# Convolution input panels multiplied in the wide form: one 512-column product with the high weights in place of two of 256 columns

## What is computed

```python
def short_conv_mixer(h, w_in, w_conv, w_out):      # h: 256 x 1024, w_in: 1024 x 3072
    b_gate, c_gate, v = jnp.split(h @ w_in, 3, axis=-1)
    u = c_gate * v
    conv = causal convolution of u over 3 tokens, per channel, taps w_conv
    return (b_gate * conv) @ w_out
...
for i in range(DEPTH):                              # two layers
    mod = silu(c) @ ada_w[i] + ada_b[i]             # shifts, scales and gates
    h = modulate(x, tok_norm[i], sh1, sc1)
    x = x + g1 * (short_conv_mixer(h) if i == 0 else mla_mixer(h))
    h = modulate(x, ch_norm[i], sh2, sc2)
    x = x + g2 * peer_mixer(h)
```

## Time and profile before

| | us |
|---|---|
| median of 3 runs | 1879.51 |
| lowest and highest | 1877.51, 1880.39 |
| the profiled execution's own time | 1876.5 |
| its span | 1874.7 |
| TensorE busy | 1855.6 (99%) |
| VectorE busy | 1448.8 (77%) |
| GpSimd busy | 1044.1 (56%) |
| ScalarE busy | 999.7 (53%) |

### The profile page before, as it was taken

How to read it: one execution, slowest core, us unless ns; L and a number is a source line. 1 busy time by engine, 2 the same in 40 slices (tenths; PEclk the granted TensorE clock), 3 DMA queues, 4 the chain that set the end, 5 groups by cost and what they waited for, 6 DMA issues and landing times.

```text
span 1874.7 us, 37387 instructions
## 1 busy us (share of the span) xinstructions
PE 1855.6 (99%) x12430; PEld 1645.0 (88%) x12430; DVE 1448.8 (77%) x2801; ACT 999.7 (53%) x1580; POOL 1044.1 (56%) x506
## 2 busy tenths in 40 slices
PE   8999999999999999999999999999999999999998
PEld 7999999888888888887789999988888888888887
DVE  6757998899878977797765489977887678666866
ACT  4354565555555555554455645555555555555553
POOL 3877557767776776100063575677787777773000
PEclk8999999999999999999999999999999999999999
DMA  8987657889888988887633576567787778777764
GB/s 349 361 271 251 209 136 190 229 227 247 234 237 231 277 231 240 252 277 232 230 103 96 179 238 192 137 160 189 179 203 189 190 188 219 189 191 214 230 189 139
DMA packets 222024, 399.45 MB, mean 213 GB/s; under 512 B 84192, under 2 KB 131680, under 8 KB 221536
## 3 DMA queue, kind: packets, MB, share of 16 engines
q1 hardware_dynamic: 137856, 383.21, 63.3%
q0 software_dynamic: 55296, 0.22, 7.1%
q10 hardware_dynamic: 28768, 14.68, 2.7%
HBM read 382.11 MB, written 15.93 MB: 212 GB/s over the span
## 4 chain that ended last, share of the span: by engine, by line
PE 92%; DVE 3%; DMA 2%; ACT 1%; POOL 1%; issue 1%; DVEq 0%; SPq 0%; ACTq 0%; POOLq 0%
PE bank L680 37%; PE bank L665 18%; PE bank L670 10%; PE bank L644 6%; PE bank L649 6%; PE bank L645 6%; PE bank L711 1%; PE bank L699 1%; DMA raw<-in_panels 1%; POOL w_lo L1387 1%; PE bank L727 1%; PE bank L509 1%; DMA raw<-in_v_panels 1%; PE bank L529 1%; PE bank L966 1%
## 5 line engine op out<-in xcount | busy, mean ns | idle before, releaser
L1418 POOL DMA_INDIRECT gates_of_tile<-g_t,place x384 | 765.9, 1995 | 324.0 <-DMA gates_of_tile<-g_t,place 147.6
L1025 ACT CAST w_hi<-raw 128x1024 fp32r<-128x1024 f32 (+1 forms) x603 | 630.5, 1046 | 354.0 <-DMA raw<-in_v_panels 119.5
L1443 DVE TENSOR_TENSOR w_lo<-raw,w_hi 128x1024 fp32r<-128x1024 f32 x488 | 597.2, 1224 | 234.0 <-PE bank L680 114.3
L1387 POOL TENSOR_TENSOR w_lo<-raw,w_hi 128x1024 fp32r<-128x1024 f32 (+2 forms) x115 | 273.1, 2379 | 323.1 <-PE bank L680 179.3
L665 PE MATMUL bank<-act_two,w_hi 128*128 128x512 f32 x1536 | 379.4, 389 | 0.0
L665 PEld LDWEIGHTS bank<-act_two,w_hi 128*128 128x128 f32 x1536 | 288.4, 188 | 59.7
L680 PE MATMUL bank<-w_hi,wt_hi 128*128 128x512 f32 x1024 | 324.4, 397 | 1.8 <-DVE wt_lo L1705 0.9
L680 PE MATMUL bank<-w_lo,wt_hi 128*128 128x512 f32 x1024 | 318.0, 391 | 0.0
L680 PE MATMUL bank<-w_hi,wt_lo 128*128 128x512 f32 x1024 | 317.2, 390 | 0.0
L644 PE MATMUL bank<-act_two,w_hi 128*128 128x256 f32 x984 | 246.4, 288 | 0.0
L645 PE MATMUL bank<-act_two,w_hi 128*128 128x256 f32 x984 | 241.2, 283 | 0.0
(11 more groups left out here) (259 smaller groups left out, 1902.5 us busy)
## 6 DMA issues: line engine op xcount, KB each, us to landing
raw<-in_u_panels SPq DMA_DIRECT2D x256, 512.0 KB, 4.1
raw<-in_v_panels SPq DMA_DIRECT2D x256, 512.0 KB, 4.0
raw<-in_panels SPq DMA_DIRECT2D x81, 512.0 KB, 4.4
ada<-in_ada_rows SPq DMA_DIRECT2D x56, 512.0 KB, 4.8
arena<-in_ada_rows SPq DMA_DIRECT2D x40, 512.0 KB, 7.2
gates_of_tile<-zero ACTq DMA_DIRECT2D x2, 4096.0 KB, 22.6
arena<-gates_of_tile SPq DMA_DIRECT2D x32, 256.0 KB, 4.3
gates_of_tile<-g_t,place POOLq DMA_INDIRECT x384
```

Source lines behind the costliest of these rows:

```text
L1025: nc.scalar.copy(w_hi[:, slot, 0:width], raw[:, slot, 0:width]).then_inc(hi_done, 1)
L1387: pool.tensor_tensor(w_lo[:, lo_slot, 0:width], raw[:, slot, 0:width], w_hi[:, slot, 0:width].bitcast(F32), ALU.subtract).then_inc(lo_done, 1)
L1418: pool.indirect_dma_start(grid, bass.IndirectOffsetOnAxis(place[:, n:n + 1], 0), kept[:, n:n + 1], None, compute_op=ALU.add).then_inc(adde ...
L1443: dve.tensor_tensor(w_lo[:, lo_slot, 0:width], raw[:, slot, 0:width], w_hi[:, slot, 0:width].bitcast(F32), ALU.subtract).then_inc(lo_done, 1)
```

## The change

Panels 2 to 23 of the input product go through a new `wide_conv_panel`: with the high weights 8 matmuls of 512 columns in place of 16 of 256, and the low weights as before. The product is now in two halves of a bank. ScalarE copies the second half to a buffer `conv_lo` (two slots of 128x256, in a part of `ring_g` that nothing else uses at this stage), **behind** the cast of panel p+3, and VectorE adds the first half to it, which releases the bank. Two of each three products had been multiplied straight out of the bank; these now need an add and then the multiply.

```diff
@@ -180,6 +180,7 @@
 
         sq = arena[:, 0:2048]
         c_sb = arena[:, 2048:2048 + T]
+        conv_lo = ring_g[:, 5120:5632].rearrange("p (e n) -> p e n", e=2)
         conv_t = arena[:, 3072:3072 + T]
         sq_sum = arena[:, 3328:3328 + T]
 
@@ -293,6 +294,7 @@
         by_gain = sem("x_by_gain_ready")
         x_ready = sem("x_ready")
         sq_ready = sem("squares_ready")
+        conv_lo_ready = sem("conv_low_half_copied")
         sum_ready = sem("square_sums_ready")
         rms_ready = sem("rms_ready")
         rstd_ready = sem("token_rstd_ready")
@@ -653,6 +655,23 @@
 
                 pe.wait_ge(pan_read[l], nth)
                 hi_then_lo(bank[:, 0:T], stage, j, norm_act)
+
+            def wide_conv_panel(j):
+
+                hi_slot, lo_slot, _, n = ring("conv_in", j)
+                bank = PAN[j % 2]
+                pe.wait_ge(evac["conv_in"], j + 1)
+                pe.wait_ge(hi_done, n)
+                for k in range(KB):
+                    w, a = slice(k * P, (k + 1) * P), slice(k * T, (k + 1) * T)
+                    pe.matmul(bank[:, 0:2 * T], w_hi[:, hi_slot, w], act_two[:, :, a], start=(k == 0), stop=False,
+                              skip_group_check=True)
+                pe.wait_ge(lo_done, n + RAW)
+                for k in range(KB):
+                    w, a = slice(k * P, (k + 1) * P), slice(k * T, (k + 1) * T)
+                    mm = pe.matmul(bank[:, 0:T], w_lo[:, lo_slot, w], act_hi[:, a], start=False, stop=(k == KB - 1),
+                                   skip_group_check=True)
+                mm.then_inc(pan_done, 1)
 
             def wide_u_panel(l, stage, j, unroll, it, nth, bank):
 
@@ -1006,7 +1025,7 @@
             busy(PAN[0], 50)
             first_pair(norm_hi, norm_ready, 0, lambda p: wait_panel("conv_in", p), fill=5)
             for j in range(2, 24):
-                full_panel("conv_in", j)
+                wide_conv_panel(j)
             conv_pair()
             for j in range(2, 8):
                 full_panel("conv_out", j, acts=conv_act)
@@ -1255,7 +1274,11 @@
             for it in range(2):
                 for b in range(4):
                     for j in range(3):
-                        split_hi("conv_in", 12 * it + 3 * b + j + HI_LEAD)
+                        p = 12 * it + 3 * b + j
+                        split_hi("conv_in", p + HI_LEAD)
+                        if p > 1:
+                            act.wait_ge(pan_done, ring("conv_in", p)[3] + HI)
+                            nc.scalar.copy(conv_lo[:, p % 2, :], PAN[p % 2][:, T:2 * T]).then_inc(conv_lo_ready, 1)
                     if it == 0:
                         conv_high(b)
             act.wait_ge(pan_done, ring("conv_in", 23)[3] + HI)
@@ -2037,13 +2060,24 @@
 
                     if b:
                         ada_row(15 + 3 * b, 12, it, 3 * b - 1)
-                    wait_product("conv_in", 12 * it + 3 * b)
-                    dve.tensor_copy(c_sb, PAN[3 * b % 2][:, 0:T]).then_inc(evac["conv_in"], 1)
+                    p = 12 * it + 3 * b
+                    if p == 0:
+                        wait_product("conv_in", p)
+                        dve.tensor_copy(c_sb, PAN[p % 2][:, 0:T]).then_inc(evac["conv_in"], 1)
+                    else:
+                        dve.wait_ge(conv_lo_ready, p - 1)
+                        dve.tensor_tensor(c_sb, PAN[p % 2][:, 0:T], conv_lo[:, p % 2, :], ALU.add).then_inc(evac["conv_in"], 1)
                     ada_row(16 + 3 * b, 12, it, 3 * b)
                     dve.drain()
-                    wait_product("conv_in", 12 * it + 3 * b + 1)
-                    dve.tensor_tensor(u_pad[:, 2:2 + T], PAN[(3 * b + 1) % 2][:, 0:T], c_sb, ALU.mult
-                                      ).then_inc(evac["conv_in"], 1)
+                    p += 1
+                    if p == 1:
+                        wait_product("conv_in", p)
+                        dve.tensor_tensor(u_pad[:, 2:2 + T], PAN[p % 2][:, 0:T], c_sb, ALU.mult).then_inc(evac["conv_in"], 1)
+                    else:
+                        dve.wait_ge(conv_lo_ready, p - 1)
+                        dve.tensor_tensor(conv_t, PAN[p % 2][:, 0:T], conv_lo[:, p % 2, :], ALU.add).then_inc(evac["conv_in"], 1)
+                        dve.drain()
+                        dve.tensor_tensor(u_pad[:, 2:2 + T], conv_t, c_sb, ALU.mult)
                     dve.drain()
                     tap = lambda i: vec[:, it * 4 + V_CONV + i * KB + b:it * 4 + V_CONV + i * KB + b + 1]
                     dve.tensor_scalar(conv_t, u_pad[:, 0:T], tap(0), None, ALU.mult)
@@ -2057,9 +2091,11 @@
                         if b == 3:
                             ada_row(15 + 12, 12, it, 11)
                     dve.drain()
-                    wait_product("conv_in", 12 * it + 3 * b + 2)
-                    dve.tensor_tensor(conv_ps[4 * it + b], PAN[(3 * b + 2) % 2][:, 0:T], conv_t, ALU.mult
-                                      ).then_inc(evac["conv_in"], 1)
+                    p += 1
+                    dve.wait_ge(conv_lo_ready, p - 1)
+                    dve.tensor_tensor(c_sb, PAN[p % 2][:, 0:T], conv_lo[:, p % 2, :], ALU.add).then_inc(evac["conv_in"], 1)
+                    dve.drain()
+                    dve.tensor_tensor(conv_ps[4 * it + b], c_sb, conv_t, ALU.mult)
                     dve.drain()
                     dve.sem_inc(conv_gated, 1)
                     if end:
```

## The result

| | us |
|---|---|
| before, median of 4 runs | 1879.95 (1877.51 to 1881.15) |
| with the change, median of 4 runs | 1891.36 (1890.11 to 1891.89) |
| ratio, 95% interval | 1.0059 [1.0043, 1.0074] |
| the profiled execution of the change | 1891.85, span 1890.1 |

The change makes the kernel 11.4 us slower. The forecast was slower, at 1884.5 with a range to 1888.5: the direction is right, the loss is more than twice the one forecast, and the time lies outside the range.

A forecast was written before the change was run, and what follows sets the result against it. TensorE was taken to bound the kernel, DMAs and GpSimd close behind. Terms +3.5 +1.2 +0.5 -0.2 = +5.0 us took the profiled execution from 1876.5 to 1881.5, the median to 1884.5; range 1880.0 to 1888.5.

The forecast's parts named there:

- TensorE's part: On TensorE over 22 input panels: wide panels take 2.77 us against 2.88, gaining 2.4 us if nothing waits.
- The first wait, panel 4: At panel 4's bank: release waits for cast, copy and add until 53.95, so panel 6 starts 1.1 us later than before.
- L: Time from issue to landing of a panel's DMA: 8.2 us for panel 7, 7.7 taken for the second half.
- The prediction's own sign: TensorE idle about 1.5 us before panel 6's first wide matmul; if absent, the panel 4 step and forecast are wrong.
- The second, panel 5: At panel 5's bank: with the added multiply VectorE frees it at 57.85, so panel 7 starts 2.2 us late.
- The turn in the first half: ScalarE and VectorE ring, 8.7 us per three panels: panel 10 stays 2.2 us late, panel 13 is 3.5 late; +3.5 us.
- The second half: Panels 13 to 22: ring through SyncE's DMA issue, cast, copy and add loses 0.8 us per six panels; +1.2 us.
- GpSimd: GpSimd's subtractions beside 15 new multiplies of two SBUF tiles: each stops GpSimd up to 0.36 us; +0.5, ends 0 and 1.5.
- The clock: Rival: TensorE's pauses drop its clock to 1.2 GHz, 2.4 us more per panel, a few making 1892; chance 0.03.
- The end: At `conv_pair`: TensorE's 0.44 us wait for GpSimd goes, 0.3 us of the last gated block shows; together -0.2 us.
- Rival 3: GpSimd becomes the bound: pauses of 0.36 us on each of 22 subtractions, DMA loads of 9.6 us; +9, 1888.5; chance 0.10.

The follow-up runs named there:

- both edits: The change with the second and third products' sums written to PSUM and ScalarE's copy put ahead of the cast; median 1880.98 us, ratio 0.9996.
- row moved: The kernel with both edits, and block 3's second ada row done behind the gated block, after the third add; median 1880.25 us, ratio 0.9994.
- narrow, two steps in PSUM: The kernel before, narrow matmuls kept, VectorE first copying second and third products from the bank to PSUM, then multiplying; median 1882.16 us, ratio 1.0009.
- the narrow form in two steps: The kernel before, narrow matmuls kept, VectorE copying second and third products out, then multiplying; 1891.52 us with the copy in SBUF, 1882.16 in PSUM.

## Why the prediction was right in direction and wrong in size

- **"TensorE's part"**, -2.4 us: right. Panels that don't wait start 2.79 us apart (2.77 was set), and the kernel with the wide matmuls alone is 2.5 us faster. The rule of "TensorE: Matmul & The Clock Gate" of the Trainium skill, section Back-to-back issue gap, by which the prediction worked out 0.5 us, is not what these rows show; the page gives it for an isolated matmul and says itself that it misses the spacing in a stream of weight loads and matmuls, such as this one.
- **"The first wait, panel 4"**: the mechanism is there, as ScalarE's row at 52.56 shows, but panel 6 came only 0.3 us late against the wide pace, not the 1.5 (53.95 against 52.4) of the text. L was 7.25 us (issued at 44.34, landed at 51.6), not 8.2: the load was not fixed by what lay before it. The prediction's own sign, idle time of TensorE before panel 6, is all but absent: 0.14 us (53.30 to 53.44), not 1.5. By its own words the step on panel 4 is wrong in size.
- **"The second, panel 5"**: in the run with the sums in PSUM panel 7 starts 3.74 us behind panel 6, 0.95 late, near the 1.1 that the text added. In the change it was 3.36, of which 2.66 - 0.43 = 2.23 is one multiply.
- **"The turn in the first half" and "The second half"**, +3.5 and +1.2: near in sum, and that in part by luck. With the sums in PSUM, panel 13 starts 34.91 us after panel 2, 3.2 more than before, and the whole stretch is 4.1 longer, against 4.7. But the parts come in other places than set. Against the kernel before, panel 7 is 0.5 us late and not 2.2, and panel 10, which was to stay as it was, loses 0.9 more. The turn of block 3, with its extra ada row, has the 1.66-us wait before panel 13, the largest of that run. That kernel's median, 1885.47, is close to the 1884.5 forecast: the forecast fits the change without the lock.
- **"GpSimd"**, +0.5 with ends 0 and 1.5: **this step failed**, in direction and in size. It read the earlier trace rows as a pause of GpSimd under VectorE's instruction. It is that only for the one that comes second. Here the second is nearly always VectorE, since a subtraction runs for 2.4 of each 2.9 us and a multiply for 0.43. GpSimd lost 0.1 us, once; VectorE lost 10.85 us in the profiled execution, and as its multiply stands ahead of the next release, the stretch is 7.4 us longer than without these waits, with what they did to the clock. No rival of the prediction has VectorE waiting. Its price in place of +0.5 is the most of the miss. The earlier trace rows shows only the one direction, but a bound for the other could be had from its durations: one whole subtraction, 2.4 us, on each of 15 multiplies, 36 us in all, and at even odds of where one falls some 15 x 0.83 x 1.2 = 15 us of VectorE's time (2.4 of 2.9 us busy, half a subtraction left on average; an estimate from those rows).
- **"The clock"** (rival 4, chance 0.03): it happened once, with a wait of 3.08 us before panel 7, and cost 5.28 - 2.79 = 2.5 us there, about the 2.4 a panel of the text, and 0.4 at panel 8; that rival set a few such panels. Waits of up to 1.86 us elsewhere in the stretch were not followed by it. Without the 2.23 us that one multiply lost, that wait would have been 0.85 us. The 1892 of this rival is near the time measured by luck: it has a few slow panels and no lock.
- **"The end"**, -0.2: wrong, a loss of 1.6 us. From the first matmul of `conv_pair` to the first add of VectorE into `xT` were 5.64 us before (105.30 to 110.94) and are 7.22 now (117.47 to 124.69), with 0.88 us of wait at 120.02 for the last bank. Most of this is the lock again: with the sums in PSUM, and as many instructions, it is 5.92 us, while it is 7.23 with only the copy moved.
- **Rival 3** gave 9 us, for another reason: GpSimd did not become the bound, and the DMAs fell from 349 to 298 GB/s.
- Two slips in the working change little: 57.85 - 55.74 is 2.1 us, not 2.2, and the chances of a loss above 1883.3 add up to 0.5 + 0.10 + 0.03 = 0.63, not 0.61.

SBUF — State Buffer of the Trainium skill, section Who interferes with whom, says that a VectorE instruction with two SBUF inputs contends with a GpSimd instruction that reads SBUF, that the shared port pair is an exclusive lock, and that the order of issue decides who blocks. The traces agree: 0.43 against 2.66 us for VectorE here, 2.41 against 3.81 for GpSimd in the earlier trace rows. The prediction used a page that only says that there is contention, and took one side of it.

**What stays open.** The kernels with both edits and with the row moved have a stretch 1.4 and 2.2 us shorter than before, but no shorter median. The times scatter by more than that, and the record shows with what: the granted clock of the execution. The 60 executions of the kernel before took 1878.0 us on average at a clock of 0.995 (15 of them) and 1883.3 at 0.992 (8). The profiled ones show where it comes from. From the first wide panel of the mixing stage of layer 0 to that of layer 1, which none of the edits touches, they took 933.9 us (before), 934.8 (the change), 934.2 (wide matmuls alone) and 934.5 (row moved), each with a clock of 0.98 between 930 and 1110 us; 938.0 and 938.8 (sums in PSUM, both edits), with 0.96; and 944.9 (narrow, two steps in PSUM; the slowest of its 11 executions), with 0.92. At the same clock the two kernels with both edits are a little faster: 1877.1 at 0.995 (5 executions) and 1881.5 at 0.992 (11), 0.8 and 1.7 us below the kernel before. A straight line through times and clocks of each batch puts the gain at 1.3 us (standard error 0.4 and 0.5). That is an estimate of mine from the runs on record, and it says that a part at least of the shorter stretch reaches the end. Why the clock between 930 and 1110 us differs from one execution to the next is open. Whether a form in which VectorE adds the halves without ScalarE's copy would do better was not tried.

## What to carry to other kernels

Before an operand of a two-tensor VectorE instruction is moved from PSUM to SBUF, look at what GpSimd does at that time: with one operand in PSUM the instruction ran beside it untouched in every run, with both in SBUF it waited for the end of GpSimd's instruction, and here that made a change of +5 us (1885.47 against 1880.28) one of +11. On an engine that works in order, a copy that releases a TensorE bank goes ahead of anything that waits for a DMA. Where TensorE is busy for 99%, work moved to a neighbour has to be priced by the delay of the next release, not by its own microseconds.

## What the runs showed of the hardware

- A 128x256 multiply of two SBUF tiles on VectorE waits for the end of GpSimd's running instruction with SBUF inputs and ends 0.28 to 0.30 us after it, up to 2.66 us in place of 0.43; cutting GpSimd's instruction in two cut the longest to 1.50. With one input in PSUM the same multiply takes 0.43 us while the subtraction runs. GpSimd's instruction is not slowed when it came first; the one that began 0.17 us after a multiply took 2.53 us, not 2.41. I had expected the reverse.
- Waits of 3.08 us (the change) and 2.12 us (the subtraction in two) on TensorE came with the lower clock, 0.50, for most of the panel behind them (5.28 and 4.37 us in place of 2.79); those of up to 1.86 us in the change, and of up to 1.75 in the runs with only the copy moved or the narrow form in two steps, did not. In the first of these the clock fell within the wait, at 58 to 59 us.
- A wide panel takes 2.79 us: with 0.95 for its eight 256-column matmuls, as in the earlier trace rows, the 512-column ones are 0.23 us each.
